# Saving x in pieces, and the order of work inside gated heads, in a two-layer fp32 trunk

## The reference, cut to what matters

```python
for l in range(DEPTH):                       # 2 layers, x is (1, 1024, 1024), f32
    h = rmsnorm(x, norm_g[l, 0]) * (1 + sc1) + sh1
    y = even_mixer(...) if l == 0 else odd_mixer(...)
    x = x + (1 + g1) * rmsnorm(y, norm_g[l, 1])
    h = rmsnorm(x, norm_g[l, 2]) * (1 + sc2) + sh2
    y = (silu(h @ w_gate) * (h @ w_up)) @ w_down
    x = x + (1 + g2) * rmsnorm(y, norm_g[l, 3])

def odd_mixer(h, ...):                       # 4 gated heads, dk = 128, dv = 256
    proj = h @ w_in                          # q, k, v, r and a rank-16 gate
    log_a = log_sigmoid(glr @ w_g2 + b_g2) / 16
    # per chunk of 64 tokens, with a state carried from chunk to chunk
    b = cumsum(log_a)
    attn[i, j] = sum_k q[i, k] * exp(b[i, k] - b[j, k]) * k[j, k]   (j <= i)
    o = attn @ v + (q * exp(b)) @ state
    state = exp(b_last) * state + (k * exp(b_last - b)).T @ v
    return (rmsnorm(o, head_g) * silu(r)) @ w_out
```

## Time and profile before

| | |
|---|---|
| time, 3 runs | median 2803.67 us (2803.15 to 2813.23) |
| the profiled execution | 2809.4 us, its span 2807.6 us |
| PE busy | 2626.0 us, 94% of the span |
| DVE, ACT, POOL busy | 1173.9, 1031.9, 1006.2 us |
| DMA | 296.32 MB, mean 106 GB/s |
| saves of x | 2 of 2048 KB, median 11.9 us from issue to landing |
| weight loads | 370 of 512 KB, median 3.5 us |

### The profile page before, as it was taken

One profiled execution on the slowest core, in us unless ns is written; L12 is line 12 of the kernel. 1 busy time (PEld: TensorE's weight loads), 2 busy tenths in 40 slices (PEclk: granted clock), 3 DMA queues, 4 the chain that ended last, 5 costly groups with the idle time before them and its releaser, 6 DMA issues.

```text
span 2807.6 us, 34984 instructions
## 1 busy us (share of the span) xinstructions
PE 2626.0 (94%) x12488; PEld 2147.5 (76%) x12488; DVE 1173.9 (42%) x1617; ACT 1031.9 (37%) x1676; POOL 1006.2 (36%) x436
## 2 busy tenths in 40 slices
PE   5999899989999999999997988887999999999997
PEld 3777777777788888888886877766878888888885
DVE  7566655541520154210555545556452015410045
ACT  3455444343432234322332335445443223422222
POOL 0111110004544444444443433333544444444443
PEclk8999999999999999999998989998999999999998
DMA  6233322234222323222237621113222222223223
GB/s 251 76 107 105 113 93 96 83 120 150 89 91 97 97 97 98 91 97 97 98 109 250 210 91 46 67 48 117 75 90 95 97 93 96 98 97 97 97 95 107
DMA packets 92068, 296.32 MB, mean 106 GB/s; under 512 B 9728, under 2 KB 10048, under 8 KB 91968
## 3 DMA queue, kind: packets, MB, share of 16 engines
q1 hardware_dynamic: 91968, 295.00, 31.1%
HBM read 272.95 MB, written 22.02 MB: 105 GB/s over the span
## 4 chain that ended last, share of the span: by engine, by line
PE 49%; issue 31%; POOL 10%; DVE 4%; ACT 2%; DMA 1%; DVEq 1%; SPq 0%; POOLq 0%; ACTq 0%
PE ps L628 10%; PE ps L632 10%; PE ps L629 10%; POOL w_lo L547 8%; PE ps L776 3%; PE ps L966 3%; PE ps L969 3%; PE ps L972 3%; PE ps L742 2%; PE ps L763 2%; DMA x<-xT 1%; POOL ybuf L558 1%; POOL arena L558 1%; PE ps L845 1%; DMA w_raw<-weights 1%
## 5 line engine op out<-in xcount | busy, mean ns | idle before, releaser
L547 POOL TENSOR_TENSOR w_lo<-w_raw,w_hi 128x1024 fp32r<-128x1024 f32 x370 | 903.6, 2444 | 1735.2 <-ACT w_hi L1036 945.4
L628 PE MATMUL ps<-h_hi,w_hi 128*128 128x512 f32 x2184 | 869.0, 398 | 30.8 <-ACT w_hi L1036 17.2
L629 PE MATMUL ps<-h_lo,w_hi 128*128 128x512 f32 x2184 | 857.6, 393 | 0.0
L1036 ACT ACTIVATE w_hi<-w_raw 128x1024 fp32r<-128x1024 f32 x290 | 306.6, 1058 | 676.1 <-PE ps L632 363.3
L632 PE MATMUL ps<-h_hi,w_lo 128*128 128x512 f32 x2184 | 540.9, 390 | 0.0
L628 PEld LDWEIGHTS ps<-h_hi,w_hi 128*128 128x128 f32 x2184 | 414.5, 190 | 133.5 <-issue 25.2
L629 PEld LDWEIGHTS ps<-h_lo,w_hi 128*128 128x128 f32 x2184 | 414.7, 190 | 86.7 <-issue 2.4
L632 PEld LDWEIGHTS ps<-h_hi,w_lo 128*128 128x128 f32 x2184 | 411.1, 188 | 85.7
L1909 DVE TENSOR_TENSOR arena<-arena,ps 128x512 f32 (+1 forms) x88 | 60.6, 688 | 778.2 <-PE ps L632 778.2
L1924 DVE TENSOR_TENSOR a_lo<-arena,a_hi 128x512 fp32r<-128x512 f32 x88 | 205.6, 2336 | 206.7 <-ACT a_hi L1420 206.7
L1406 ACT ACTIVATE arena<-ps 128x512 f32<-128x512 f32 x88 | 52.7, 599 | 323.6 <-PE ps L632 323.6
(11 more groups left out here) (205 smaller groups left out, 2617.0 us busy)
## 6 DMA issues: line engine op xcount, KB each, us to landing
w_raw<-weights SPq DMA_DIRECT2D x370, 512.0 KB, 3.5
arena<-ada_w SPq DMA_DIRECT2D x80, 512.0 KB, 3.6
arena<-ada_w SPq DMA_DIRECT2D x8, 1024.0 KB, 14.9
x<-xT SPq DMA_DIRECT2D x4, 2048.0 KB, 13.5
proj<-stage SPq DMA_DIRECT2D x12, 512.0 KB, 3.5
x_d<-x SPq DMA_DIRECT2D x2, 2048.0 KB, 11.9
arena<-proj SPq DMA_DIRECT2D x8, 512.0 KB, 3.7
x<-x_d SPq DMA_DIRECT2D x2, 2048.0 KB, 12.2
```

Of the source, the lines that this page charges most:

```text
L547: pool.tensor_tensor(w_lo[:, s, :], w_raw[:, s, :], w_hi[:, s, :].bitcast(f32), ALU.subtract).then_inc(lo_done, 1)
L628: pe.matmul(bank(b), w, high[:, k, :], start=k == 0, stop=False)
L629: pe.matmul(bank(b), w, low[:, k, :], start=False, stop=False)
L1036: a.activation(w_hi[:, slot, :], w_raw[:, slot, :], ACT.Copy).then_inc(hi_done, 1)
```

## The change

1. `save` moves out of `project` and takes a half and a block number: it saves two blocks of one half, 512 KB. Half 0 goes out in layer 0, second token half of the FFN, behind each of the first four pairs of down units. Half 1 goes out in `project` behind the stores of pairs 4 to 7. Readers wait for 64 and 128 instead of 16 and 32.
2. POOL: the split of late unit 3 stands behind difference 3, that of unit 4 behind difference 6.
3. PE: late unit 2 is done in parts of 18 and 6 matmuls behind j = 0 and 1; unit 3 in six parts of 4 behind j = 2 to 7.
4. ACT: the copies of v stand behind levels 1 and 2, those of ke behind 5, the eviction of unit 2 and rounding of unit 4 (unit of the output projection in the last head) behind 3. Silu stands behind the root of the outputs.
5. DVE: ke behind level 1, qe behind level 2, each with its own semaphore. `masked` for the levels is one instruction over the second halves of the groups alone (8 x 64 columns); the diagonal stays two instructions. `g_pred` counts 9 a head instead of 16.

```diff
@@ SP @@
+            def save(half, k):
+                sp.wait_ge(x_part, 4 * upd(0, 3, half))
+                t = slice(half * HALF, (half + 1) * HALF)
+                sp.dma_start(x_d[:, k:k + 2, t], x[:, k:k + 2, t]).then_inc(x_saved, 16)
...
-                for i in range(1, 5):
+                with sp.Fori(1, 5) as i:
                     body(i)
                     store(i - 1)
-                    if i % 3 == 1:
-                        save(i // 4)
-                with sp.Fori(5, PAIRS_IN) as i:
+                for i in range(5, 9):
+                    body(i)
+                    store(i - 1)
+                    save(1, 2 * i - 10)
+                with sp.Fori(9, PAIRS_IN) as i:
                     body(i)
                     store(i - 1)
...
-                    stream(PACK_FFN[layer], use, FFN_UNITS // 2)
+                    if (layer, half) == (0, 1):
+                        stream(PACK_FFN[0], use, FB)
+                        for i in range(4):
+                            stream(PACK_FFN[0] + 2 * FB + 2 * i, use + 2 * FB + 2 * i, 1)
+                            save(0, 2 * i)
+                        stream(PACK_FFN[0] + 2 * FB + 8, use + 2 * FB + 8, FB // 2 - 4)
+                    else:
+                        stream(PACK_FFN[layer], use, FFN_UNITS // 2)
@@ POOL head @@
                     differences(h, lv)
-                    if lv == 1:
+                    if lv == 3:
                         late(h, 3)
-                    if lv == 4 and not last:
-                        late(h, 4)
                 if not last:
+                    late(h, 4)
                     late(h, 5)
@@ PE head @@
-                        pe.wait_ge(g_pred, 16 * h + 2 * max(0, j - 1) + 1)
+                        if j > 1:
+                            pe.wait_ge(g_pred, 9 * h + j + 1)
...
-                            late(h, 2, 0, 10)
+                            late(h, 2, 0, 18)
...
-                        elif j < 3:
-                            late(h, 2, 4 + 6 * j, 10 + 6 * j)
-                        elif j == 3:
-                            late(h, 2, 22, 24)
-                            late(h, 3, 0, 4)
-                        elif j < 7:
-                            late(h, 3, 6 * j - 20, 6 * j - 14)
+                        elif j == 1:
+                            late(h, 2, 18, 24)
                         else:
-                            late(h, 3, 22, 24)
+                            late(h, 3, 4 * j - 8, 4 * j - 4)
@@ ACT head @@
-                        if lv < 2:
-                            copy_v(2 * lv)
-                            copy_v(2 * lv + 1)
-                        if lv == 3:
+                        if 0 < lv < 3:
+                            copy_v(2 * lv - 2)
+                            copy_v(2 * lv - 1)
+                        if lv == 5:
...
-                        if lv == 4:
+                        if lv == 3:
                             late_evict(h, 2, gvr[:, 0, HALF:S])
...
-                    a.drain()
-                    a.wait_ge(g_r, 16 * h + 16)
-                    a.activation(gvr[:, :, :], gvr[:, :, :], ACT.Silu).then_inc(g_silu, 1)
                     load_sqrt()
...
                     a.activation(ms, ms, ACT.Sqrt, bias=eps_c, scale=1.0 / C_DV).then_inc(g_root, 1)
+                    a.wait_ge(g_r, 16 * h + 16)
+                    a.activation(gvr[:, :, :], gvr[:, :, :], ACT.Silu).then_inc(g_silu, 1)
@@ DVE head @@
+                            m = 128 >> j
+                            late_half = lambda t: t.rearrange("p n (c u t) -> p n c u t", u=2, t=m)[:, :, :, 1, :]
+                            got = ps[:, 1024 * (j % 2):1024 * (j % 2) + 1024].rearrange("p (n i) -> p n i", i=P)
+                            v.copy_predicated(late_half(attnT), late_half(masks[:, j - 1:j, :]).broadcast_to([P, 8, 64 // m, m]),
+                                              late_half(got)).then_inc(g_pred, 1)
...
-                        if lv == 0:
+                        if lv == 1:
+                            v.wait_ge(g_ek, h + 1)
+                            v.tensor_tensor(ke, ke, gk, ALU.mult).then_inc(g_k_done, 1)
+                        if lv == 2:
                             v.wait_ge(g_eb, 2 * h + 2)
-                            v.tensor_tensor(qe, qe, gq, ALU.mult).then_inc(g_qk_done, 1)
-                            v.wait_ge(g_ek, h + 1)
-                            v.tensor_tensor(ke, ke, gk, ALU.mult).then_inc(g_qk_done, 1)
+                            v.tensor_tensor(qe, qe, gq, ALU.mult).then_inc(g_q_done, 1)
```

More of the change, by code:

```diff
@@ L399, in body @@
                     ada_pair(ada0 + i)
-                def save(half):
-                    sp.wait_ge(x_part, 4 * upd(0, 3, half))
-                    t = slice(half * HALF, (half + 1) * HALF)
-                    sp.dma_start(x_d[:, :, t], x[:, :, t]).then_inc(x_saved, 16)
                 body(0)
-                for i in range(1, 5):
+                with sp.Fori(1, 5) as i:
                     body(i)
                     store(i - 1)
-                    if i % 3 == 1:
-                        save(i // 4)
-                with sp.Fori(5, PAIRS_IN) as i:
+                for i in range(5, 9):
[3 more added lines that the diff above has]
+                with sp.Fori(9, PAIRS_IN) as i:
                     body(i)
@@ L908, in head @@
                         if j == 3:
[L909 removed]
+                            pe.wait_ge(g_k_done, h + 1)
                             pe.wait_ge(g_vtr, 4 * h + 4)
@@ L915, in head @@
                                 mm.then_inc(g_kt, 1)
-                    pe.wait_ge(g_pred, 16 * h + 16 + 1)
+                    pe.wait_ge(g_pred, 9 * h + 9 + 1)
                     pe.wait_ge(g_ktr, 2 * h + 2)
+                    pe.wait_ge(g_q_done, h + 1)
                     for n in range(8):
@@ L1089, in write_h @@
                 if k == 0 and norm == (1, 0, 1):
-                    a.wait_ge(x_saved, 16)
+                    a.wait_ge(x_saved, 64)
                 elif k == 0:
@@ L1484, in h_low @@
                 if (layer, kind, half, k) == (1, 0, 1, 0):
-                    v.wait_ge(x_saved, 32)
+                    v.wait_ge(x_saved, 128)
                 if kind == 1:
@@ L1779, in masked @@
                         v.sem_inc(waited, 1)
-                        mask = (j - 1) % (LEVELS + 1)
-                        for n in range(2):
-                            v.copy_predicated(attnT[:, 4 * n:4 * n + 4, :],
-                                              masks[:, mask:mask + 1, :].broadcast_to([P, 4, P]),
-                                              bank(2 * (j % 2) + n).rearrange("p (n i) -> p n i", i=P)).then_inc(g_pred, 1)
+                        if j == 0:
+                            for n in range(2):
+                                v.copy_predicated(attnT[:, 4 * n:4 * n + 4, :],
+                                                  masks[:, LEVELS:LEVELS + 1, :].broadcast_to([P, 4, P]),
+                                                  bank(n).rearrange("p (n i) -> p n i", i=P)).then_inc(g_pred, 1)
+                        else:
+                            m = 128 >> j
[3 more added lines that the diff above has]
+                                              late_half(got)).then_inc(g_pred, 1)
                     v.tensor_tensor(chunk(ke), chunk(gb)[:, :, P - 1:P].broadcast_to([P, 8, P]), chunk(gb), ALU.subtract).then_inc(g_ekd, 1)
```

5 lines of the change are left out of this document (2 added, 3 removed).

## The result

The changed kernel takes 2766.55 us (median of 4 runs, 2761.75 to 2767.59), beside 2805.19 of the kernel before: ratio 0.9854, 95% interval 0.983 to 0.9877. In a second comparison it was 2768.28 beside 2809.78, ratio 0.9845 (0.9832 to 0.9858). So 38.6 and 41.5 us less, where 53.0 were forecast; 2750.7 was 16 us too low. The time lies within the range given (2736 to 2778), above the forecast's own stretch (2741 to 2762). The profiled execution of after took 2767.59 us (span 2765.8), 41.8 less than that of before.

What follows compares the result with a forecast made beforehand. TensorE was taken as the bound, busy nearly throughout, with gains only where it waits or runs at low clock. Projection 17.4 plus heads 35.6 gave 53.0 off 2803.67: 2750.7 us, range 2736 to 2778.

Steps and rivals of the forecast that it cites:

- rival C: Layer 1's projection: traffic is the limit, the pieces of x do nothing useful, waits only move; 2768 us, chance 0.10.
- rival A: Level stage gives back what it gets: 3 to 4 us a head instead of 8.7; 2772 us, chance 0.17.
- Part 1, what stays (6.0): Layer 1's projection: stalls at units 4, 8 and 10 keep 6.0 of 23.4 us lost, so 17.4 come back.
- under 2 us: Sign of a right forecast: TensorE's wait at the projection's second unit pair falls below 2 us.
- no low clock at 1490 and 1530: Sign of a right forecast: TensorE no longer runs at low clock at these two times in layer 1's projection.
- The cover of 4 us: Quiet part of the projection: loads land 4 us before needed, against 1.7 to 3 us for a piece; no cost.
- Part 2, the level stage (8.7): Gated heads: a walk through head 1's new order puts the first output product at 1777.2, not 1785.88; 8.7 us a head.
- Rival D: Level stage: masked copy on every second column group is expensive; up to 64 us more, 2815 us, chance 0.05.
- thin 0.6: Level stage walk: level 3's products end only 0.6 us earlier than before, an argument for the level stage giving back its gain.
- GpSimd (POOL) explains both: Head 1: GpSimd's splits of late units 3 and 4 explain TensorE's waits of 5.16 and 4.25 us.
- Part 3 (1.1 a head, last head 3.8): Outputs: silu behind them lets evictions start earlier; 1.1 us in each of heads 0 to 2, 3.8 in the last.
- Last head, level stage (3.6): Last head: its level stage falls from 38.1 to 34.5 us like the others, 3.6 us.

Runs made afterwards that it cites:

- e2: The kernel before with only the save of x changed (pieces and new places), heads as before: 2797.70 us, ratio 0.9959.
- e3: The changed kernel with x saved as before in two 2 MB transfers, level stage and silu as changed: 2779.87 us, ratio 0.9890.
- e1: The changed kernel run again with no edit: 2768.28 us, ratio 0.9845 to the kernel before.
- e11: The changed kernel with x saved in two 2 MB transfers at the places of the pieces: 2764.29 us, ratio 0.9847.
- e5: The changed kernel with GpSimd's order of before (splits of late units 3 and 4 behind differences 1 and 4): 2763.47 us, ratio 0.9839.
- e9: The changed kernel with ScalarE's level-stage order of before, GpSimd's as changed: 2765.12 us, ratio 0.9845.
- e10: The changed kernel with both ScalarE's and GpSimd's orders of before in the level stage: 2774.69 us, ratio 0.9887.
- e12: The changed kernel with GpSimd splitting late unit 4 behind level 6's products and unit 3 behind difference 1 again: 2753.60 us, ratio 0.9810.
- e6: The changed kernel with silu and its drain ahead of the outputs again: 2777.26 us, ratio 0.9880.
- e7: The changed kernel with SyncE issuing unit 2i+2's weight load ahead of ada pair i and store i-1 in the projection: 2780.73 us, ratio 0.9899.

## Why the prediction was right, and where not

The range and the sign held; the size was 53.0 against 41.8 by the profiles. The measured 2766.55 lies above the 2741 to 2762 that had the chance of 0.50, and next to the 2768 of rival C and the 2772 of rival A; the time alone would not have told them apart, e2 and e3 did. The 11.2 are: projection 3.9, heads 0 to 2 1.4, last head and what is behind it 1.1 (5.1 against 6.2), and 4.8 in stretches that the change doesn't set (the start of the projection and the way to the heads).

- **Part 1, what stays (6.0).** Mis-sized: 9.9 stay (13.5 of 23.4 came back). Units 4 and 10 are where I put them, with stalls of 2.73 and 2.68 for 1.7 and 2.6; unit 8 has none of over 0.2 for 1.7. What I left out is the clock: both stalls are followed by the low level (0.79), which I had priced behind the long stalls only. How it falls out changes from one execution to the next: in e1, the same kernel, unit 8 has the longest stall, 3.81. Over ten executions with the same order of issue there are 5.1 to 7.5 us of waits in two or three places, and projections of 144.3 to 148.0. So of the signs named, "under 2 us" and "no low clock at 1490 and 1530" failed; loads of at most 8 us (7.7) held.
- **Part 1, why.** "Cuts the half-1 save into four pieces" carries nothing by itself (e11); taking half 0 away and half 1 to the quiet part does. The cover of 4 us that I counted for a piece is about enough for the whole 2 MB.
- **Part 2, the level stage (8.7).** 7.2 measured in head 1. My walk holds within 0.1 us up to the last level's products; it is at the last scores that 1.5 us are missed: they began 0.72 us behind level 6's products, held by a late piece, and the masked copy behind them took 1.30 and not 0.7 (that of level 5 took 1.31, but was over 1.17 us before the last began). Rival D (strided copies dear) was so true at two of seven levels, and rival A's thin 0.6 held.
- **Part 2, the cause.** The step "GpSimd (POOL) explains both" failed as an attribution. It saw that the split ahead of difference 5 itself waited for ScalarE, but counted only on the split's new place and gave ScalarE's moves no term; by the medians the runs show two remedies for one stall (e5, e9, e10). What the rest of the stage's gain comes from stays open, as said at e10. And the 2.1 us that level 0 gained is mostly given back by level 2, where the same split now stands (e12).
- **Part 3 (1.1 a head, last head 3.8).** Mis-sized low. From before to after the outputs became 1.4 shorter in each of heads 0 to 2, and the gate ahead of heads 1 and 2 another 1.2 and 1.1 by the early table load, a term that the working doesn't have. Undone alone (e6) part 3 costs 3.1, 3.0 and 1.8. In the last head the stretch from the first output product to the root went from 17.4 to 11.7, 5.7 for 3.8: the 17.3 of the working was right, its 13.5 was not, since the evictions start at +2.4 and not at +3.2 and the second follows the first after 0.8. The 1.2 lost on the high halves of h came as worked out (1.24 behind the turns; e6 has it back).
- **Last head, level stage (3.6).** Only 0.6. Of the 2.9 that are missing (37.4 for 34.5), 1.4 is what heads 0 to 2 miss as well (35.9), and 1.5 the low clock behind the wait of 2.34 us (that behind 2.78 was made up again), a term that my walk at full clock didn't have; parts 2 and 3 together still came to 5.1 for 6.2.

That periods came out nearly as predicted (28.0 for 29.4) thus hides two errors of opposite sign: in head 1 the level stage gave 1.5 less than worked out (7.2 for 8.7), and the rest of the period, 9.7 - 7.2 = 2.5, was 1.4 more than the 1.1 of part 3 (1.1 of it the table load, 0.3 the outputs). That they nearly cancel is luck.

## What to carry to other kernels

When a stall has two engines in its chain (a split that waits for another engine's half), undo each edit alone and then both, before you name the cause: here either alone cost nothing in the median, and both 12 us by the ratios. On two engines that lock each other out, look for work inside the chain that nobody needs yet and move it out behind it; moving it about within the chain was worth 1 us, moving it out 2.2 a head. A save or prefetch on a shared queue is best judged by its place: 2 MB in a quiet stretch cost no more than four pieces there, while in the busy stretch each 2 MB save had a stall of 8.5 to 9.2 us behind it (e3).

## What the runs showed of the hardware that was not expected

- The predicated copy of 128x512 with its inner run of 64 down to 4 elements takes 0.70 to 0.74 us; with runs of 2 and 1 it takes 1.31 and 1.30. The half product with a run of 1 stays at 0.69.
- Stalls of nearly the same length do and don't bring TensorE's low level, at the same place of the program too: before level 2's scores of head 1, 2.84 us in after didn't and 2.85 in e9 did (scores of 3.78 for 2.05); before unit 10, 2.68 in after did (products of 0.63 for 0.39) and 2.97 in e10 didn't (first fence e9, second e10):

```profile
1737.48 3.78 PE L895 MATMUL ps<-arena 128*128 128x128 f32 x16 [2.85 <-DVEq L1802]
```
```profile
1518.45 0.47 PE L637 MATMUL ps<-h_hi,w_hi 128*128 128x512 f32 x1 [2.97 <-ACT w_hi L1042]
1518.76 0.40 PE L638 MATMUL ps<-h_lo,w_hi 128*128 128x512 f32 x1
```

- The engines' work up to the projection is the same in all fourteen executions, and it began between 1454.6 and 1461.3 us: a spread of 6.7 us, as much as many an edit is worth. It arises ahead of the last 120.0 us, which are the same in all. In the first 200 us the granted clock was 0.96 where it began at 1454.6 (before) and 1454.7 (e7), and 0.93 where it began at 1459.2 (after) and 1461.3 (e6).
- A table load (1.28 us) is free where its engine waits anyway. With silu last it moved ahead of Abs within the loop, for 1.2 and 1.1 us, and not in the head that is written out, where the order of functions is the same.
